# Order of the split products and GpSimd's share of the low weights in the first output projection

## The chip, the cores and the metric

One core of a Trainium2 chip runs the whole program. The metric is the device time of one execution in microseconds (us), as the median of several runs.

## What is computed

The reference is a chain of three blocks over 1024 tokens of width 1024. The change lies at the end of the first block, in its output projection and what follows it:

```python
y = jnp.concatenate([y_conv, y_ret], axis=-1) @ w_out[l]      # 1024 x 2048 by 2048 x 1024
h = h + gate * y
...
return _rmsnorm(h, final_g)
...
h = layer_norm(x, ln_in_g, ln_in_b)                           # first line of the second block
```

All of it is in float32. The kernel gets float32 accuracy out of a faster matmul format (`fp32r`, here F32R) by splitting each operand x in a high part, x rounded to F32R, and a low part, x minus the high part. A product is then the sum of three: high by high, high by low, low by high.

## The kernel before

The stage is `out_sync`, `out_tensor`, `out_scalar` and `out_vector`, one function for each engine's queue. The 2048 rows of `w_out` are taken in 16 pieces of 128 rows (NK = 16), the retention half first (`K_ORDER`). The tokens are 8 tiles of 128, in three groups: (0, 1, 2), (3, 4, 5), (6, 7). Each token tile has a pair of PSUM banks for its 128 x 1024 sum, so only three can be open, and the weights are read once for each group.

A step i of group g multiplies one piece of weights with the group's tokens. `products` (line 369) issues three matmuls for a token and half of the columns, so a step has 18 matmuls in the first two groups and 12 in the third: 768 in all. There are 48 steps, but the last two pieces of a group are kept for the first two steps of the next. So 44 rows of weights are fetched and split, numbered s = 16g + i - 2g. Rows 0 to 15 serve the first group, 14 to 29 the second, 28 to 43 the third.

A row n passes through four engines:
- SyncE fetches it into `wo_raw[:, n % 2]` (line 1306), one of two slots, once the low part of row n-2 is made.
- ScalarE makes `wo_hi` (line 1422) when the row has landed and TensorE is done with row n-2 (`wo_used`).
- VectorE makes `wo_lo` (line 1293, `out_lows`) from `wo_raw` and `wo_hi`.
- TensorE waits at the start of the step for `wo_lo` of its row, and so has the high part too.

In the first group ScalarE and VectorE also split the activations (lines 1424 and 1298).

When a token's sum is complete (`o1_mm`), VectorE multiplies it with the gate into `tmp` (line 1474) and adds it to the residual in `xo` (line 1476). The first step of the next group writes over the banks, each token's after the `tmp` that read it (`gate_ok`). ScalarE takes squares (1450), VectorE normalises: lines 1479, 1483, 1485 for the first norm and the statistics of the second, 1489 and 1494 for centring and scaling. These run beside the next group's steps. Between them VectorE calls `out_lows(dve, upto)`, and ScalarE `highs(upto)`, at places written out by hand. The order of the work on each engine is this order in the code. In steps 10, 11 and 12 of a group TensorE also transposes the finished tokens of the group before (line 1358). ScalarE (1431) and VectorE (1500) take them out of the bank as high and low part for the second block, and SyncE stores the tokens (1313) and loads new residuals (1309) in between.

GpSimd does nothing in this stage. Its next work is `ch_lo` (line 1690), the low part of the weights of the second block's first projection. TensorE's first product of it (`channel`) follows right behind the last step.

## Time and profile before

| | |
|---|---|
| runs | 2764.33, 2764.53, 2764.77 us; median 2764.53 |
| profiled execution | span 2763.9 us from the first to the last instruction; what its run took in all is not listed, the median stands 0.6 us above its span |
| TensorE busy | 2689.4 us, 97% of the span |
| VectorE, ScalarE, GpSimd busy | 2086.6, 1069.2, 477.0 us |
| the stage | first matmul with `wo_hi` at 849.9, first product of the next stage at 1042.2 |

Matmuls overlap in the trace: one is listed with 0.39 us and the next begins 0.23 us later. Starts are more telling than durations.

### The profile page before, as it was taken

Reading aid. Unit: us, or ns where it says so; the run is one execution under the profiler, and the core shown is the slowest. Engines: PE = TensorE matmul, PEld = TensorE weight load, DVE = VectorE, ACT = ScalarE, POOL = GpSimd, SP = SyncE. Lnnn points to the kernel's source line nnn. Section 1 sums busy time; section 2 is a strip of 40 time slices with the busy share of each in tenths; the row PEclk is TensorE's granted clock in tenths of the full one; section 3 lists DMA queues with packets and bytes.
Section 4 is the critical chain, followed back from the end, with each engine's and each line's share of the span. In section 5 each row is a group of like instructions: output and inputs, shape, how many; then the busy total and the mean of one; then the engine's idle time right before and its main releaser. Section 6 shows DMA issues by size and latency. Waiting matters only on the chain.

```text
span 2763.9 us, 33573 instructions
## 1 busy us (share of the span) xinstructions
PE 2689.4 (97%) x13192; PEld 2199.6 (80%) x13192; DVE 2086.6 (75%) x2796; ACT 1069.2 (39%) x1599; POOL 477.0 (17%) x254
## 2 busy tenths in 40 slices
PE   6999999999999999999999999999999999999998
PEld 5888888888888878778875678888887888888887
DVE  6999998873724663369998886688186988887978
ACT  5111112243413332245537751365232554555332
POOL 0000000000100002001210001354211656655000
PEclk8999999999999999999999999999999999999999
DMA  5312222224325452011101032100132222225431
GB/s 223 116 63 69 94 97 61 84 92 142 99 107 175 136 176 90 31 62 39 47 30 36 32 123 96 46 31 23 62 115 80 96 77 89 87 77 188 170 99 61
DMA packets 97710, 250.18 MB, mean 91 GB/s; under 512 B 7361, under 2 KB 34369, under 8 KB 96018
## 3 DMA queue, kind: packets, MB, share of 16 engines
q1 hardware_dynamic: 93010, 231.49, 24.4%
q10 hardware_dynamic: 4288, 15.73, 1.5%
q8 instruction: 105, 1.72, 0.2%
q0 software_dynamic: 256, 0.82, 0.1%
q14 instruction: 51, 0.42, 0.1%
HBM read 202.92 MB, written 45.09 MB: 90 GB/s over the span
## 4 chain that ended last, share of the span: by engine, by line
PE 80%; DVE 14%; issue 2%; ACT 1%; DMA 1%; DVEq 0%; ACTq 0%
PE pair L370 16%; PE pair L372 16%; PE pair L371 16%; PE pair L3657 7%; PE pair L3242 5%; PE pair L3244 5%; PE pair L3245 5%; DVE counted L1942 3%; PE pair L2593 2%; DVE reached L1993 1%; PE pair L2156 1%; DVE top_i L1999 1%; PE pair L1754 1%; PE pair L2172 1%; PE pair L2185 1%
## 5 line engine op out<-in xcount | busy, mean ns | idle before, releaser
L370 PE MATMUL pair<-u_hi,w_hi 128*128 128x512 f32 x768 | 302.1, 393 | 1.2 <-PEq L92 0.9
L641 DVE SCALAR_TENSOR_TENSOR conv_acc<-aT,cols,conv_acc 128x1024 f32<-128x1024 f32 x232 | 297.9, 1284 | 6.7
L371 PE MATMUL pair<-u_lo,w_hi 128*128 128x512 f32 x768 | 300.3, 391 | 0.0
L372 PE MATMUL pair<-u_hi,w_lo 128*128 128x512 f32 x768 | 300.3, 391 | 0.0
L370 PEld LDWEIGHTS pair<-u_hi,w_hi 128*128 128x128 f32 x768 | 145.2, 189 | 32.7 <-issue 2.4
L371 PEld LDWEIGHTS pair<-u_lo,w_hi 128*128 128x128 f32 x768 | 145.0, 189 | 30.6 <-issue 0.7
L372 PEld LDWEIGHTS pair<-u_hi,w_lo 128*128 128x128 f32 x768 | 145.0, 189 | 30.6
L370 PE MATMUL pair<-h_hi,ch_hi 128*128 128x512 f32 x392 | 153.8, 392 | 2.8 <-ACT ch L1824 2.6
L372 PE MATMUL pair<-h_hi,ch_lo 128*128 128x512 f32 x392 | 152.7, 389 | 0.0
L371 PE MATMUL pair<-h_lo,ch_hi 128*128 128x512 f32 x392 | 152.6, 389 | 0.0
L1014 POOL TENSOR_TENSOR yrT<-yrT,gate_c 128x1024 f32<-128x1024 f32 x8 | 18.9, 2366 | 758.1 <-ACT yrT L907 758.1
L3192 POOL TENSOR_TENSOR op_lo<-w_sum,op_hi 128x512 fp32r<-128x512 f32 x80 | 137.6, 1721 | 33.6 <-ACT op_hi L3322 33.6
L454 DVE TENSOR_TENSOR w_lo<-wt,w_hi 128x1024 fp32r<-128x1024 f32 (+1 forms) x64 | 69.8, 1091 | 77.0 <-ACT w_hi L450 76.9
L3242 PE MATMUL pair<-t_hi,op_hi 128*128 128x512 f32 x320 | 124.6, 389 | 0.0
L3245 PE MATMUL pair<-t_hi,op_lo 128*128 128x512 f32 x320 | 124.5, 389 | 0.0
L3244 PE MATMUL pair<-t_lo,op_hi 128*128 128x512 f32 x320 | 124.5, 389 | 0.0
L1690 POOL TENSOR_TENSOR ch_lo<-wt,ch_hi 128x1024 fp32r<-128x1024 f32 x17 | 40.7, 2395 | 464.7 <-ACT ch_hi L1648 464.7
L450 ACT ACTIVATE w_hi<-wt 128x1024 fp32r<-128x1024 f32 (+1 forms) x64 | 60.8, 950 | 142.8 <-PE pair L372 135.3
L1293 DVE TENSOR_TENSOR wo_lo<-wo_raw,wo_hi 128x1024 fp32r<-128x1024 f32 x44 | 54.0, 1228 | 66.5 <-ACT wo_hi L1422 66.4
L370 PE MATMUL pair<-h_hi,p_hi 128*128 128x512 f32 x256 | 103.6, 405 | 0.0
L372 PE MATMUL pair<-h_hi,p_lo 128*128 128x512 f32 x256 | 100.2, 392 | 0.0
L371 PE MATMUL pair<-h_lo,p_hi 128*128 128x512 f32 x256 | 99.7, 389 | 0.0
(510 smaller groups left out, 7105.1 us busy)
## 6 DMA issues: line engine op xcount, KB each, us to landing
wt<-in_w_ch SPq DMA_DIRECT2D x60, 512.0 KB, 3.4
wo_raw<-in_w_out SPq DMA_DIRECT2D x44, 512.0 KB, 3.6
wt<-in_w_up SPq DMA_DIRECT2D x10, 1024.0 KB, 4.9
w_raw<-in_w_up SPq DMA_DIRECT2D x10, 1024.0 KB, 4.8
g_spill<-g_stage SPq DMA_DIRECT2D x40, 256.0 KB, 2.2
ada_mod<-in_ada_mod SPq DMA_DIRECT2D x4, 2048.0 KB, 14.3
wt<-in_w_conv SPq DMA_DIRECT2D x16, 512.0 KB, 3.5
qk<-qk_st SPq DMA_DIRECT2D x8, 1024.0 KB, 6.4
```

Of the source, the lines that this page charges most:

```text
L370: nc.tensor.matmul(bank, w[0], x[0], start=(first and k == 0), stop=False)
L371: nc.tensor.matmul(bank, w[0], x[1], start=False, stop=False)
L372: return nc.tensor.matmul(bank, w[1], x[0], start=False, stop=(last and k == n_k - 1))
L450: nc.scalar.activation(slot_view(w_parts[0], n), slot_view(wt, n), ACT.Copy).then_inc(job_hi, 1)
L454: nc.vector.tensor_tensor(slot_view(w_parts[1], n), slot_view(wt, n), slot_view(w_parts[0], n).bitcast(F32), ALU.subtract).then_inc(job_lo, 1)
L641: nc.vector.scalar_tensor_tensor(dst, x, w, conv_acc[:], ALU.mult, ALU.add).then_inc(conv_step, 1)
L1942: nc.vector.tensor_scalar(to, scores(t), least, None, op, ALU.add, accum_out=found[:, t - 2:t - 1]).then_inc(counts_ok, 1)
L3192: nc.gpsimd.tensor_tensor(op_lo[j], operand(w, j), op_hi[j].bitcast(F32), ALU.subtract).then_inc(op_lo_ok, 1)
L3242: nc.tensor.matmul(bank, hi[:, k, :], x_hi[:, k, :], start=(j in opens and k == 0), stop=False, skip_group_check=True)
L3244: nc.tensor.matmul(bank, hi[:, k, :], x_lo[:, k, :], start=False, stop=False, skip_group_check=True)
L3245: last = nc.tensor.matmul(bank, lo[:, k, :], x_hi[:, k, :], start=False, stop=(k == 3), skip_group_check=True)
L3657: last = nc.tensor.matmul(dn_bank(p, t), x[:, i, t * P:(t + 1) * P], w[:, i, :], start=(p in (P1, P7, P2) and c == kind == i == 0), stop=( ...
```

## The change

Three things are changed:
- In a step TensorE waits for the high part alone. It issues the products with `wo_hi` of all tokens (high and low activations), then waits for the low part, then issues the products with `wo_lo` of all tokens. In the first step of a group this is done token by token.
- The low parts of rows 16 to 29, and of the odd rows 31 to 43, are made by GpSimd (`out_gpsimd`) in place of VectorE, with a semaphore of their own. SyncE waits for the one or the other before it fetches into the slot.
- ScalarE and VectorE take the transposed tokens out of the bank one row of weights earlier.

```diff
--- before.py
+++ after.py
@@ -1284,14 +1284,24 @@
         def x_parts(k):
             return yc_parts if k < KT else yr_parts
 
+        wo_low_pool = sem("o1_wlo_pool")
+
+        def on_pool(n):
+            return NK <= n < NK + NEW or (n >= NK + NEW and n % 2 == 1)
+
+        def wo_low(n):
+            made = sum(on_pool(m) == on_pool(n) for m in range(n + 1))
+            return (wo_low_pool if on_pool(n) else wo_lo_ok), made
+
         at_low = [0]
 
         def out_lows(dve, upto):
             for n in range(at_low[0], min(upto, N_SPLITS)):
                 k = K_ORDER[n % NK]
-                dve.wait_ge(wo_hi_ok, n + 1)
-                nc.vector.tensor_tensor(wo_parts[1][:, n % 2, :], wo_raw[:, n % 2, :],
-                                        wo_parts[0][:, n % 2, :].bitcast(F32), ALU.subtract).then_inc(wo_lo_ok, 1)
+                if not on_pool(n):
+                    dve.wait_ge(wo_hi_ok, n + 1)
+                    nc.vector.tensor_tensor(wo_parts[1][:, n % 2, :], wo_raw[:, n % 2, :],
+                                            wo_parts[0][:, n % 2, :].bitcast(F32), ALU.subtract).then_inc(wo_lo_ok, 1)
                 if n < NK:
                     x = x_parts(k)
                     dve.wait_ge(x_hi_ok, n + 1)
@@ -1302,7 +1312,7 @@
         def out_sync(sp):
             def weights(n):
                 if n >= 2:
-                    sp.wait_ge(wo_lo_ok, n - 1)
+                    sp.wait_ge(*wo_low(n - 2))
                 sp.dma_start(wo_raw[:, n % 2, :], a["w_out"][:, K_ORDER[n % NK], :]).then_inc(wo_in[n % 2], 16)
 
             def residual(t):
@@ -1365,7 +1375,20 @@
                 k = K_ORDER[s % NK]
                 if g and i in (10, 11, 12):
                     transposes(3 * (g - 1) + i - 10)
-                pe.wait_ge(wo_lo_ok, s + 1)
+                x_hi, x_lo = x_parts(k)
+                w_hi, w_lo = (w[:, s % 2, :] for w in wo_parts)
+
+                def multiply(j, t, x, w):
+                    for h in range(2):
+                        last = nc.tensor.matmul(bank_of[j][:, h, :], x[:, k % KT, t * P:(t + 1) * P],
+                                                w[:, h * HALF:(h + 1) * HALF],
+                                                start=(i == 0 and x is x_hi and w is w_hi),
+                                                stop=(i == NK - 1 and w is w_lo))
+                    if i == NK - 1 and w is w_lo:
+                        last.then_inc(o1_mm, 1)
+                    return last
+
+                pe.wait_ge(wo_hi_ok, s + 1)
                 if g == 0:
                     pe.wait_ge(x_lo_ok, i + 1)
                 for j, t in enumerate(O_GROUPS[g]):
@@ -1375,12 +1398,15 @@
                         pe.wait_ge(ot_ok, KT * TT)
                     if n == 0 and j == 1:
                         pe.wait_ge(pw_out, KT - 1)
-                    for h in range(2):
-                        last = products(bank_of[j][:, h, :],
-                                        [x[:, k % KT, t * P:(t + 1) * P] for x in x_parts(k)],
-                                        [w[:, s % 2, h * HALF:(h + 1) * HALF] for w in wo_parts], i, NK)
-                    if i == NK - 1:
-                        last.then_inc(o1_mm, 1)
+                    multiply(j, t, x_hi, w_hi)
+                    multiply(j, t, x_lo, w_hi)
+                    if i == 0:
+                        pe.wait_ge(*wo_low(s))
+                        last = multiply(j, t, x_hi, w_lo)
+                if i:
+                    pe.wait_ge(*wo_low(s))
+                    for j, t in enumerate(O_GROUPS[g]):
+                        last = multiply(j, t, x_hi, w_lo)
                 if i == NK - 1:
                     pe.wait_ge(o1_mm, O_GROUPS[g][-1] + 1)
                     pe.sem_inc(wo_used, 1)
@@ -1459,8 +1485,9 @@
                 act.wait_ge(bnv_ok, tokens[-1] + 1)
                 nc.scalar.activation(sd2, mv1[:, :, 1], ACT.Sqrt, bias=eps5[:]).then_inc(sd_ok, 1)
                 for j, t in enumerate(tokens):
-                    highs(at0 + 12 + j)
+                    highs(at0 + 11 + j)
                     evacuate(t)
+                highs(at0 + 14)
                 if g == 1:
                     act.wait_ge(h2_out[2], 32)
                     channel_high(act, 0)
@@ -1516,7 +1543,7 @@
                 at0 = NEW * (g + 1)
                 if g:
                     for j, t in enumerate(O_GROUPS[g - 1]):
-                        out_lows(dve, NEW * g + 12 + j)
+                        out_lows(dve, NEW * g + 11 + j)
                         low_part(t)
                 out_lows(dve, at0 + 2)
                 add(0, tokens[0])
@@ -1683,6 +1710,13 @@
             sp.dma_start(a_row[:], a["a_bs"]).then_inc(a_in, 16)
             for n in range(10, N_CH):
                 channel_weights(sp, n)
+
+        def out_gpsimd(pool):
+            for n in range(N_SPLITS):
+                if on_pool(n):
+                    pool.wait_ge(wo_hi_ok, n + 1)
+                    nc.gpsimd.tensor_tensor(wo_parts[1][:, n % 2, :], wo_raw[:, n % 2, :],
+                                            wo_parts[0][:, n % 2, :].bitcast(F32), ALU.subtract).then_inc(wo_low_pool, 1)
 
         def mix_gpsimd(pool):
             for n in range(N_CH):
@@ -2385,6 +2419,7 @@
         @block.gpsimd
         def _(pool):
             ret_gpsimd(pool)
+            out_gpsimd(pool)
             mix_gpsimd(pool)
```

How the order of instructions moves is shown at three places. First TensorE, last step of the second group (row 29) before: its start with the first token. L370, L371 and L372 are the three products, `o1_wlo` is the semaphore of VectorE's low parts.

```order
L370 MATMUL pair<-wo_hi,yc_hi 128x512 [waits o1_wlo]
L371 MATMUL pair<-wo_lo,yc_hi 128x512
L372 MATMUL pair<-wo_hi,yc_lo 128x512
L370 MATMUL pair<-wo_hi,yc_hi 128x512
L371 MATMUL pair<-wo_lo,yc_hi 128x512
L372 MATMUL pair<-wo_hi,yc_lo 128x512
L370 MATMUL pair<-wo_hi,yc_hi 128x512
```

The same step with the change, up to the first step of the third group. `o1_whi` is the semaphore of the high parts, `o1_wlo_pool` that of GpSimd's low parts, `o1_gate` that of `tmp`.

```order
L1383 MATMUL pair<-wo_hi,yc_hi 128x512 [waits o1_whi]
L1383 MATMUL pair<-wo_hi,yc_hi 128x512
L1383 MATMUL pair<-wo_hi,yc_lo 128x512 x2
L1383 MATMUL pair<-wo_hi,yc_hi 128x512 x2
L1383 MATMUL pair<-wo_hi,yc_lo 128x512 x2
L1383 MATMUL pair<-wo_hi,yc_hi 128x512 x2
L1383 MATMUL pair<-wo_hi,yc_lo 128x512 x2
L1383 MATMUL pair<-wo_lo,yc_hi 128x512 [waits o1_wlo_pool]
L1383 MATMUL pair<-wo_lo,yc_hi 128x512 x5
L1383 MATMUL pair<-wo_hi,yc_hi 128x512 [waits o1_mm,o1_gate,o1_whi]
```

A token's six matmuls stood together; now the products with `wo_lo` of all three tokens are the last six of the step.

Second GpSimd's queue, between its last work in the stage before (`yrT`) and the next stage's `ch_lo`, before and with the change.

```order
L1014 TENSOR_TENSOR yrT<-yrT,gate_c 128x8x128 [waits x_in1,ada_in3] x8
L1690 TENSOR_TENSOR ch_lo_674<-wt,ch_hi_677 128x1024 [waits ch_hi]
L1690 TENSOR_TENSOR ch_lo_675<-wt,ch_hi_678 128x1024 [waits ch_hi]
L1690 TENSOR_TENSOR ch_lo_676<-ch_raw,ch_hi_679 128x1024 [waits ch_hi]
L1690 TENSOR_TENSOR ch_lo_674<-wt,ch_hi_681 128x1024 [waits ch_hi]
```

```order
L1014 TENSOR_TENSOR yrT<-yrT,gate_c 128x8x128 [waits x_in1,ada_in3] x8
L1718 TENSOR_TENSOR wo_lo<-wo_raw,wo_hi 128x1024 [waits o1_whi] x21
L1724 TENSOR_TENSOR ch_lo_674<-wt,ch_hi_677 128x1024 [waits ch_hi]
L1724 TENSOR_TENSOR ch_lo_675<-wt,ch_hi_678 128x1024 [waits ch_hi]
L1724 TENSOR_TENSOR ch_lo_676<-ch_raw,ch_hi_679 128x1024 [waits ch_hi]
```

The 21 low parts stand ahead of the first `ch_lo`.

Third VectorE in the third group, from row 30 on, beside the normalisation of tokens 3 and 4, before and with the change.

```order
L1293 TENSOR_TENSOR wo_lo<-wo_raw,wo_hi 128x1024 [waits o1_whi]
L1528 RECIPROCAL small_616<-small_616 128x3 [waits o1_rms]
L1479 SCALAR_TENSOR_TENSOR xo_611<-xo_611,small_616,fg_bc 128x1024 [waits o1_rr]
L1483 BN_STATS small_616<-xo_611 128x6 [waits o1_rmsx]
L1483 BN_STATS small_616<-xo_611 128x6
L1485 BN_AGGR small_616<-small_616 128x2 [waits o1_bn]
L1293 TENSOR_TENSOR wo_lo<-wo_raw,wo_hi 128x1024 [waits o1_whi]
L1479 SCALAR_TENSOR_TENSOR xo_612<-xo_612,small_616,fg_bc 128x1024
```

```order
L1303 TENSOR_TENSOR wo_lo<-wo_raw,wo_hi 128x1024 [waits o1_whi]
L1555 RECIPROCAL small_616<-small_616 128x3 [waits o1_rms]
L1506 SCALAR_TENSOR_TENSOR xo_611<-xo_611,small_616,fg_bc 128x1024 [waits o1_rr]
L1510 BN_STATS small_616<-xo_611 128x6 [waits o1_rmsx]
L1510 BN_STATS small_616<-xo_611 128x6
L1512 BN_AGGR small_616<-small_616 128x2 [waits o1_bn]
L1506 SCALAR_TENSOR_TENSOR xo_612<-xo_612,small_616,fg_bc 128x1024
```

The low part of row 31 is gone from between the two tokens.

## Rows read from the trace of the kernel before

**Rows 1.** The page: span, and TensorE's granted clock in 40 slices.

```profile
span 2763.9 us, 33573 instructions
...
PEclk8999999999999999999999999999999999999999
```

**Rows 2.** Windows: us, busy us (x instructions) per engine, clock, DMA share, GB/s.

```profile
822.00:846.00 24.00, 24.00 (x105) 19.39 (x104) 8.13 (x7) 4.97 (x5) 0.00 (x0) 1.00 0.42 145
930.00:956.00 26.00, 26.00 (x117) 21.52 (x116) 18.89 (x21) 7.70 (x8) 0.00 (x0) 1.00 0.48 133
...
985.80:1042.10 56.30, 49.39 (x217) 37.69 (x216) 42.08 (x43) 22.27 (x27) 2.41 (x1) 1.00 0.52 159
```

**Rows 3.** Waits in the third group, 985.8 to 1042.2: us, times, longest.

```profile
ACT wo_hi L1422 <- DMA wo_raw<-in_w_out: 23.6, 11, 3.5
...
PEld pair L370 <- DVE wo_lo L1293: 8.3, 8, 2.0
...
PE pair L370 <- DVE wo_lo L1293: 4.8, 7, 1.5
```

**Rows 4.** Timeline of TensorE: start, us, operation, idle before it.

```profile
916.70 0.47 PE L370 MATMUL pair<-wo_hi,yc_hi 128*128 128x512 f32 x1 [0.30 <-PE pair L372]
...
920.23 0.50 PE L370 MATMUL pair<-wo_hi,yc_hi 128*128 128x512 f32 x1 [0.55 <-DVE tmp L1474]
...
986.12 0.47 PE L370 MATMUL pair<-wo_hi,yc_hi 128*128 128x512 f32 x1 [0.30 <-PE pair L372]
...
996.61 0.50 PE L370 MATMUL pair<-wo_hi,yc_hi 128*128 128x512 f32 x1 [1.53 <-DVE wo_lo L1293]
...
1042.16 0.47 PE L370 MATMUL pair<-h_hi,ch_hi 128*128 128x512 f32 x1
```

**Rows 5.** The chain of waits in order of time: start, us, what.

```profile
983.13 1.24 DVE tmp L1474
...
985.75 1.24 DVE tmp L1474
...
995.46 1.09 DVE wo_lo L1293
...
1019.86 6.00 DMA wo_raw<-in_w_out
```

**Rows 6.** Timeline of ScalarE: high parts of rows 17, 18, 31, 33 and 43.

```profile
926.08 1.06 ACT L1422 ACTIVATE wo_hi<-wo_raw 128x1024 fp32r<-128x1024 f32 x1 [1.67 <-PE pair L372]
930.16 1.06 ACT L1422 ACTIVATE wo_hi<-wo_raw 128x1024 fp32r<-128x1024 f32 x1 [3.02 <-PE pair L372]
...
992.27 1.05 ACT L1422 ACTIVATE wo_hi<-wo_raw 128x1024 fp32r<-128x1024 f32 x1
...
1000.10 1.06 ACT L1422 ACTIVATE wo_hi<-wo_raw 128x1024 fp32r<-128x1024 f32 x1 [3.46 <-DMA wo_raw<-in_w_out]
...
1036.11 1.06 ACT L1422 ACTIVATE wo_hi<-wo_raw 128x1024 fp32r<-128x1024 f32 x1 [1.51 <-PE pair L372]
```

**Rows 7.** Timeline of SyncE: fetches of rows 33 and 43.

```profile
996.58 0.33 SPq L1306 DMA_DIRECT2D wo_raw<-in_w_out  x1
...
1032.09 0.33 SPq L1306 DMA_DIRECT2D wo_raw<-in_w_out  x1
```

**Rows 8.** Timelines of ScalarE, GpSimd and VectorE around the first `ch_lo` operations.

```profile
1031.61 1.05 ACT L1648 ACTIVATE ch_hi<-wt 128x1024 fp32r<-128x1024 f32 x1
...
1032.74 2.41 POOL L1690 TENSOR_TENSOR ch_lo<-wt,ch_hi 128x1024 fp32r<-128x1024 f32 x1 [255.27 <-ACT ch_hi L1648]
1043.19 2.41 POOL L1690 TENSOR_TENSOR ch_lo<-wt,ch_hi 128x1024 fp32r<-128x1024 f32 x1 [8.05 <-ACT ch_hi L1648]
...
1043.31 1.23 DVE L1474 TENSOR_TENSOR tmp<-pair,gate_bc 128x1024 f32<-128x1024 f32 x1
1044.57 2.11 DVE L1476 TENSOR_TENSOR xo<-xo,tmp 128x1024 f32<-128x1024 f32 x1
```

## Prediction

> **What bounds the kernel now.** I read the page first: TensorE is busy nearly everywhere and its clock is granted in full, 2.4 GHz, outside the first slice [rows 1]. So a gain has to come from moments in which TensorE waits, and a loss from new ones. The change touches one stage, 849.9 to 1042 us. The windows by group of tokens come next [rows 2]: in the third group TensorE is busy 49.4 of 56.3 us. A step of three tokens takes 4.08 us, read off ScalarE's pace in the second group, 926.08 to 930.16 [rows 6], so a matmul costs 4.08/18 = 0.227 us. The second group waits for nothing once it runs.
>
> The list of waits of the third group [rows 3] names two limits. TensorE waits for VectorE's low weights, 8.3 us in 8 waits on its weight-load side, and ScalarE's high parts wait for the weights' DMA, 23.6 us in 11 waits. The chain of waits [rows 5] shows how they join. It runs through VectorE's additions from 983.13 on, through its normalisation with a low part in it at 995.46, and later through transfers of `wo_raw` such as the one of 6.00 us at 1019.86. A row n can be fetched only when the low part of row n-2 is made, since both use one slot of `wo_raw`. One turn of a slot is therefore fetch, high part, low part, and two slots alternate. Undisturbed a turn costs 3.5 + 1.1 + 1.2 = 5.8 us [rows 6 to 8], while TensorE needs a slot every 2 x 12 x 0.227 = 5.4 us in the third group and every 8.2 us in the second. In the third group the loop of a slot is the bound, not the moment at which TensorE looks at the low part.
>
> **The change part by part.** The sum is made against the profiled execution, whose span is 2763.9 us. The median of the runs is 2764.5, so 0.6 us lie around the span, and a difference carries over unchanged.
>
> (1) High products first in a step. The matmuls are as many as before. In the steady second group it gives nothing, as TensorE does not wait there. It costs something in the last step of a group. Before, the first token's sum is complete after 6 matmuls of that step; now after 12 + 2 = 14, since the low products of all tokens come last. VectorE's additions begin 8 x 0.227 = 1.8 us later.
> - Into the second group: TensorE's third token starts at 920.23 on the release by VectorE's `tmp` [rows 4], and VectorE needs 2.6 us for each addition pair (983.13 to 985.75, [rows 5]) against TensorE's 1.36 for a token. That start moves by the whole **1.8 us**, and the second group has no slack to take it up.
> - Into the third group: the same again. TensorE starts at 986.12 [rows 4] and would reach its second token at 987.6. VectorE's second `tmp` ends at 985.75 + 1.2 + 1.8 = 988.8, so TensorE loses 1.2. ScalarE's high part of row 31, at 992.27 [rows 6], stands behind the squares of the added rows and moves by the whole **1.8 us**.
>
> (2) GpSimd makes the low parts of the second group (rows 16 to 29). I cost this at nothing. What covers it: fetch 3.5, hand-over and high part 1.1, GpSimd 2.4 make 7.0 us a turn, against 8.2 that TensorE takes. Where stores share the DMA queues a landing takes up to 6.0 [rows 5] and the turn 9.5; the start of a step may then be 1.3 late against a slack of 2.9 (4.08 less the high part). If that cover were gone it would cost about 1 us in each of two or three steps.
>
> (3) GpSimd makes the odd rows 31 to 43. The odd slot makes six turns from the high part of row 31 (992.27) to that of row 43 (1036.11), 43.8 us [rows 6]. Of these the six landings take 3.5 three times, then 4.3, 5.8 and 4.0, 24.6 in all (first and last: 996.58 to 1000.10 and 1032.09 to 1036.11, [rows 6, 7]). The rest, 19.2 us, is high parts, low parts and VectorE being late, as with row 31: high part done at 993.3, low part at 995.4. With GpSimd the rest is per turn 1.13 from the high part's start to GpSimd's (1031.61 to 1032.74), 2.41 for the operation, and 0.03 to the issue: six times 3.57 = 21.4 [rows 8].
> To this comes a wait that the trace shows in its reverse. VectorE's `xo`, two operands in SBUF, takes 2.11 instead of 1.23 us at 1044.57 and ends where GpSimd's operation, begun at 1043.19, has ended (1045.60) plus 1.1 [rows 8]. So these exclude each other. GpSimd's wait is between 0 and one VectorE operation, 1.2 to 1.3. I take 0.2 per turn, 1.1 us in all, since VectorE is on such operations half of the first turns only and nearly idle in the later ones. Sum 22.5 - 19.2 = **3.3 us** later at row 43. I keep the landings as they are, because the stores and loads beside them remain. If all came in 3.5 the sum falls by 3.6; if the three late ones took 6.0 it grows by 3.9.
> The Trainium skill (GPSIMD Engine Reference, section Elementwise — side-by-side cycle accounting) gives an fp32 addition of 2048 elements as 4497 ns, so as an estimate 2.25 us for 1024. By that figure six turns would be 1.0 us shorter; the trace's own 2.41 for this very shape is used instead.
>
> (4) The end. Before, 6.05 us pass from row 43's high part to the channel products at 1042.16 [rows 4, 6], TensorE being the limit. After, the same queue of GpSimd holds row 43's low part and then `ch_lo` of the next stage: 1.13 + 2.41 + 2.41 + 0.05 = 6.0. So **0**, but with GpSimd in TensorE's place.
>
> (5) VectorE gives up 21 low parts of 1.14 to 1.23 us, up to three of which are now in the chain before 1011. They would bring the even slot forward by 2 to 3 us. Worth nothing, as the odd slot comes last. The earlier evacuations on ScalarE are also worth nothing: TensorE's transposes are followed by work that does not need them.
>
> (6) Pitch of the matmuls. The new order alternates between two banks and stationary matrices. Before, pitches differ between stages by some 3% without a wait: 105 matmuls in 24 us and 117 in 26 [rows 2]. Over 768 matmuls that is 5 us. I take none, since the operands are the same as in the nearest row, and put it into the range.
>
> Sum: 1.8 + 1.8 + 3.3 + 0 = 6.9; the second loss of 1.2 in (1) lies beside the second 1.8. Less a little, because TensorE's last step starts nearer to its data: **6.7 us slower**, 2771.2. All that follows hangs on the transposes behind this stage, so nothing takes it up.
>
> **The rivals.**
> - Handover only (0.20): the landings come in 3.5 as the slot's fetches are spread, or VectorE's lateness in the odd slot was larger than I think. Then 6.7 - 3.6 = 3.1: 2767.6, which is no measurable change. For it: the uncontended landings are all 3.5. Against: the stores still stand beside rows 39 to 43.
> - Faster (0.07): what bounds the third group is only TensorE's look at the low part. It comes 8 x 0.227 = 1.8 us later in a step, and GpSimd takes VectorE's queue out of the loop, so the 8.3 us of waits vanish along with most late landings (3.6), against 3.6 for the handovers: about 8 less, 2756. It decides from the point at which a slot's turn is under 5.4 us. Against: fetch and high part alone are 4.6, and GpSimd's 2.4 make 7.0.
> - Port (0.10): each of GpSimd's operations waits for a whole VectorE operation, and VectorE's additions wait for GpSimd in turn. Six times 1.1 more: 2777.5. For it: 2.11 us for `xo` [rows 8]. Against: from 1015 on VectorE has gaps. The Trainium skill (SBUF — State Buffer, section Who interferes with whom) says that whichever of the two begins second is blocked for the whole instruction, and Perfetto Trace Analysis (section Optimizing Scalar/DVE Operations) that offloading between the two might therefore not help. By that rule this rival holds; the trace agrees with the block, but not yet with how often it strikes.
> - The change moves work but costs nothing (0.03): the handover is hidden because VectorE is sped up elsewhere. 2764.5.
>
> **How the numbers follow.** The forecast has 0.60. I count a difference below 0.2% (5.5 us), about what a measurement of this kernel can tell, as no change: 2759.0 to 2770.0. Of the forecast 0.10 falls under that line. Slower: 0.50 + 0.10 = 0.60. Same: 0.10 + 0.20 + 0.03 = 0.33. Faster: 0.07. The range goes from handover only to 3.3 above the forecast, 2767.0 to 2774.5, and leaves out the faster case, most of the port case and the unchanged one, 0.2 together.
>
> **What would show it.** The third token of the second group starts 1.8 us later than 920.23; the high part of row 31 comes 3.6 later than 992.27; six turns of the odd slot take 47 us, and TensorE's waits in the third group are for GpSimd's `wo_lo` and at the end for `ch_lo`. The channel products start near 1048.8. I am wrong if TensorE's waits in the third group sum to less than before, or if row 43's high part begins before 1039.

## The result and the profile after

| | before | change |
|---|---|---|
| runs, us | 2764.77 median of 15 (2763.94 to 2766.79) | 2770.96 median of 15 (2768.94 to 2772.00) |
| ratio | | 1.0021, 95% interval 1.0014 to 1.0028 |
| profiled execution, span | 2763.9 | 2769.2 |
| high part of row 15 (the last before the first handover) | 908.33 | 908.41 |
| first channel product | 1042.16 | 1046.39 |
| from there to the end | 1721.7 | 1722.8 |

The change is 6.2 us slower; 6.7 were forecast. Of the 5.3 us between the two spans 4.2 arise in the stage and 1.1 behind it, where the two kernels have the same code. Every profiled run whose total time is listed took 1.8 us more than its span (2771.01 and 2769.2 for the change). By the same 1.8 us, as an estimate, the profiled execution of the kernel before took 2765.7, 0.9 more than its median, which is why the spans differ by less than the medians.

The page of the change. VectorE has lost 14 us of work and GpSimd gained 54; TensorE is busy 3 us longer, and the span [rows 1] has grown by 5.3.

```profile
span 2769.2 us, 33573 instructions
...
PE 2692.5 (97%) x13192; PEld 2199.6 (79%) x13192; DVE 2072.2 (75%) x2775; ACT 1069.7 (39%) x1599; POOL 530.8 (19%) x275
```

Windows of the change: us, busy us (x instructions) per engine (PE, PEld, DVE, ACT, POOL), clock, DMA share, GB/s. The first three are the three groups of tokens [rows 2]; the last two lie 350 us behind the stage.

```profile
849.90:916.40 66.50, 65.92 (x290) 53.94 (x288) 35.15 (x31) 28.14 (x28) 0.00 (x0) 1.00 0.51 174
916.40:987.60 71.20, 68.83 (x313) 56.31 (x312) 37.83 (x30) 21.53 (x25) 34.50 (x14) 1.00 0.47 148
987.60:1048.50 60.90, 52.97 (x226) 38.89 (x226) 40.76 (x39) 24.93 (x29) 21.93 (x9) 1.00 0.48 156
1392.00:1395.60 3.60, 0.98 (x4) 0.86 (x5) 3.57 (x7) 2.47 (x4) 2.05 (x1) 1.00 0.00 0
1395.60:1399.40 3.80, 3.80 (x11) 2.97 (x10) 3.77 (x10) 2.08 (x4) 0.32 (x1) 0.55 0.00 0
```

Timeline of TensorE in the change: start, us, operation, idle before it. The third token of the second group, the third of the third group, and the first channel product [rows 4].

```profile
922.11 0.74 PE L1383 MATMUL pair<-wo_hi,yc_hi 128*128 128x512 f32 x2 [0.95 <-DVE tmp L1501]
...
990.71 0.73 PE L1383 MATMUL pair<-wo_hi,yc_hi 128*128 128x512 f32 x2 [0.91 <-DVE tmp L1501]
...
1046.39 0.50 PE L370 MATMUL pair<-h_hi,ch_hi 128*128 128x512 f32 x1 [1.14 <-POOL ch_lo L1724]
```

The third token starts 1.88 us later than 920.23. The last row names the new releaser of the next stage, GpSimd's `ch_lo`.

Timeline of ScalarE in the change: high parts of rows 15, 31, 33 and 43 [rows 6].

```profile
908.41 1.06 ACT L1448 ACTIVATE wo_hi<-wo_raw 128x1024 fp32r<-128x1024 f32 x1 [2.07 <-PE pair L1383]
...
995.95 1.05 ACT L1448 ACTIVATE wo_hi<-wo_raw 128x1024 fp32r<-128x1024 f32 x1
...
1003.11 1.06 ACT L1448 ACTIVATE wo_hi<-wo_raw 128x1024 fp32r<-128x1024 f32 x1 [3.08 <-DMA wo_raw<-in_w_out]
...
1040.47 1.06 ACT L1448 ACTIVATE wo_hi<-wo_raw 128x1024 fp32r<-128x1024 f32 x1 [1.77 <-DMA wo_raw<-in_w_out]
```

Row 31's high part is 3.68 us later than 992.27. Six turns of the odd slot take 1040.47 - 995.95 = 44.5 us instead of 43.8; 47 were forecast. Its landings, issue to high part: 3.24, 3.38, 3.35, 4.19, 4.30, 3.96, together 22.4 instead of 24.6.

GpSimd in the change: low parts of rows 31 and 35, then the first `ch_lo` of the next stage, which starts as soon as row 43's low part is out.

```profile
997.08 2.76 POOL L1718 TENSOR_TENSOR wo_lo<-wo_raw,wo_hi 128x1024 fp32r<-128x1024 f32 x1 [13.92 <-ACT wo_hi L1448]
...
1011.57 2.39 POOL L1718 TENSOR_TENSOR wo_lo<-wo_raw,wo_hi 128x1024 fp32r<-128x1024 f32 x1 [4.54 <-ACT wo_hi L1448]
...
1043.96 2.38 POOL L1724 TENSOR_TENSOR ch_lo<-wt,ch_hi 128x1024 fp32r<-128x1024 f32 x1
```

Waits of the third group in the change, 987.6 to 1048.5: us, times, longest [rows 3].

```profile
POOL wo_lo L1718 <- ACT wo_hi L1448: 43.3, 7, 13.9
ACT wo_hi L1448 <- DMA wo_raw<-in_w_out: 21.7, 12, 3.1
...
PEld pair L1383 <- POOL wo_lo L1718: 5.3, 7, 0.9
...
PEld pair L1383 <- ACT wo_hi L1448: 3.4, 6, 1.4
PEld pair L1383 <- DVE wo_lo L1303: 2.7, 3, 1.1
```

TensorE's weight loads (PEld) wait 5.3 + 3.4 + 2.7 = 11.4 us, where they waited 8.3 for VectorE alone: the wait for a low part has become one for low and high parts, and ScalarE still waits for the DMA.

### The profile page after: what moved, and what is told of

The parts are those of the page before. It is cut to its first block, busy times and chain, and to the rows that moved or that the text cites. A ratio compares the mean times of both kernels' runs of the same rounds, so it can differ in the third digit from the quotient of the medians.

```text
span 2769.2 us, 33573 instructions
## 1 busy us (share of the span) xinstructions
PE 2692.5 (97%) x13192; PEld 2199.6 (79%) x13192; DVE 2072.2 (75%) x2775; ACT 1069.7 (39%) x1599; POOL 530.8 (19%) x275
## 4 chain that ended last, share of the span: by engine, by line
PE 83%; DVE 10%; issue 2%; ACT 1%; DMA 1%; POOL 1%; DVEq 0%; ACTq 0%
PE pair L370 16%; PE pair L372 15%; PE pair L371 15%; PE pair L3692 7%; PE pair L3280 5%; PE pair L3277 5%; PE pair L3279 5%; PE pair L1383 4%; DVE counted L1976 2%; PE pair L2628 2%; PE pair L2190 1%; DVE reached L2027 1%; PE pair L1788 1%; DMA wo_raw<-in_w_out 1%; PE pair L2206 1%
## 5 line engine op out<-in xcount | busy, mean ns | idle before, releaser
L370 PE MATMUL pair<-u_hi,w_hi 128*128 128x512 f32 x768 | 302.0, 393 | 1.2 <-PEq L92 0.9
L371 PE MATMUL pair<-u_lo,w_hi 128*128 128x512 f32 x768 | 300.3, 391 | 0.0
L372 PE MATMUL pair<-u_hi,w_lo 128*128 128x512 f32 x768 | 300.1, 391 | 0.0
L370 PEld LDWEIGHTS pair<-u_hi,w_hi 128*128 128x128 f32 x768 | 145.1, 189 | 32.7 <-issue 2.4
L371 PEld LDWEIGHTS pair<-u_lo,w_hi 128*128 128x128 f32 x768 | 145.1, 189 | 31.0 <-issue 0.7
L372 PEld LDWEIGHTS pair<-u_hi,w_lo 128*128 128x128 f32 x768 | 145.0, 189 | 30.2
L370 PE MATMUL pair<-h_hi,ch_hi 128*128 128x512 f32 x392 | 154.5, 394 | 3.8 <-ACT ch L1858 2.7
L372 PE MATMUL pair<-h_hi,ch_lo 128*128 128x512 f32 x392 | 153.3, 391 | 0.0
L371 PE MATMUL pair<-h_lo,ch_hi 128*128 128x512 f32 x392 | 153.1, 391 | 0.0
L370 PE MATMUL pair<-h_hi,p_hi 128*128 128x512 f32 x256 | 103.6, 405 | 0.0
L372 PE MATMUL pair<-h_hi,p_lo 128*128 128x512 f32 x256 | 100.2, 391 | 0.0
L371 PE MATMUL pair<-h_lo,p_hi 128*128 128x512 f32 x256 | 99.6, 389 | 0.0
L370 PE MATMUL pair<-w_o_hi,h_hi 128*128 128x512 f32 x248 | 98.0, 395 | 0.2
L371 PE MATMUL pair<-w_o_lo,h_hi 128*128 128x512 f32 x248 | 96.5, 389 | 0.0
```

Source lines behind the costliest of these rows:

```text
L370: nc.tensor.matmul(bank, w[0], x[0], start=(first and k == 0), stop=False)
L371: nc.tensor.matmul(bank, w[0], x[1], start=False, stop=False)
L372: return nc.tensor.matmul(bank, w[1], x[0], start=False, stop=(last and k == n_k - 1))
```

## The experiments

Each run is compared with the kernel before on the same chip. An interval of a ratio is about 0.001 wide to each side, 2.7 us, so the medians of e3, e5 and e7 can't be told from the kernel before. So besides the medians I read each profiled execution in two pieces: **stage**, from row 15's high part to the first channel product (it takes out that executions enter up to 1.8 us apart), and **behind**, from there to the end of the span. The last two columns count the stretches in which the windows show TensorE's clock below 1.00 in each piece; the last microseconds of the span, without a matmul, are left out.

| run | median minus before, us | stage | behind | low clock in stage | behind |
|---|---|---|---|---|---|
| before / once more (e10) | 0 / 0.0 | 133.8 / 133.3 | 1721.7 / 1721.3 | 0 / 0 | 1 / 1 |
| change / once more (e9) | 6.2 / 5.7 | 138.0 / 139.8 | 1722.8 / 1723.1 | 0 / 0 | 2 / 2 |
| e1 no GpSimd | 3.6 | 135.9 | 1722.1 | 0 | 1 |
| e2 GpSimd only | 3.9 | 135.8 | 1721.8 | 0 | 1 |
| e3 last step by token | 1.6 | 135.5 | 1721.4 | 1 | 1 |
| e4 GpSimd in 2nd group only | 3.8 | 137.8 | 1724.3 | 1 | 2 |
| e5 half of GpSimd's columns | 0.0 | 132.9 | 1724.0 | 0 | 2 |
| e6 delay only | 5.5 | 137.7 | 1721.2 | 0 | 1 |
| e7 third buffer | -0.7 | 131.8 | 1722.8 | 0 | 2 |
| e8 token order, third buffer | -4.5 | 129.1 | 1723.1 | 0 | 2 |
| e11 change, third buffer | 2.8 | 134.5 | 1723.5 | 1 | 2 |
| e12 token order, two buffers | -2.8 | 132.1 | 1721.1 | 0 | 1 |

The starts of the high parts of rows 15, 31 and 43 divide the stage of each profiled execution further. The six turns between the last two are split again into landings and rest, where the two buffers alternate.

| run | row 15 to row 31, us | rows 31 to 43, six turns | of these landings | rest | row 43 to first channel product |
|---|---|---|---|---|---|
| before / once more | 83.9 / 83.9 | 43.8 / 43.3 | 24.6 / 24.1 | 19.3 / 19.1 | 6.05 / 6.07 |
| change / once more | 87.5 / 87.6 | 44.5 / 46.3 | 22.4 / 23.4 | 22.1 / 22.9 | 5.92 / 5.92 |
| e1 no GpSimd | 87.5 | 43.8 | 24.5 | 19.3 | 4.55 |
| e2 GpSimd only | 84.3 | 44.7 | 23.0 | 21.7 | 6.74 |
| e3 last step by token | 84.0 | 45.5 | 23.6 | 21.8 | 6.10 |
| e4 GpSimd in 2nd group only | 87.5 | 44.2 | 25.1 | 19.1 | 6.06 |
| e5 half of GpSimd's columns | 87.6 | 40.5 | 24.9 | 15.6 | 4.83 |
| e6 delay only | 86.6 | 45.1 | 25.9 | 19.2 | 6.10 |
| e7 third buffer | 83.9 | 41.8 | | | 6.06 |
| e8 token order, third buffer | 83.9 | 39.7 | | | 5.50 |
| e11 change, third buffer | 87.5 | 41.0 | | | 5.94 |
| e12 token order, two buffers | 83.9 | 43.5 | 24.2 | 19.3 | 4.64 |

The first column is 3.6 us longer in every run whose last steps have the low products of all tokens at the end (change, e1, e4, e5, e11). The rest of the turns is 19.1 to 19.3 us where VectorE makes the low parts of the third group, and 21.7 to 22.9 where GpSimd makes the odd ones in full.

**e1: the new order without GpSimd.** `on_pool` returns False for every row.

```diff
-            return NK <= n < NK + NEW or (n >= NK + NEW and n % 2 == 1)
+            return False
```

> The change without GpSimd: all low parts on VectorE, products and evacuations as in the change. Theory (handover and slot loop): the two handovers still delay VectorE by 1.8 us each, GpSimd's longer turns and its queue at the end are gone. The high part of row 31 starts 3.6 later than before (995.9), the channel products at 1044.2 (+2.0 against 1042.2 before, -2.2 against the change). Rival (all of the loss is GpSimd's): channel products at 1042.2 or earlier. Rival (all of it is the product order): 1046.4, as in the change.

Median 2768.93 (2767.80 to 2770.22), ratio 1.0012 (1.0003 to 1.0021). First channel product 1044.62, stage 2.3 us over the mean of before (133.5). That is less than the two delays of 1.8: both are there in full (87.5 against 83.9 to row 31), the turns are as long as before, and 1.5 us come back behind row 43's high part (4.55 against 6.05). There TensorE begins the last step on the high part, without the low one. The median moved by 3.6, 1.3 more than this one stage.

**e2: GpSimd alone**, with the products and the places of the high and low parts of before.

```diff
-                pe.wait_ge(wo_hi_ok, s + 1)
+                pe.wait_ge(*wo_low(s))
...
-                    multiply(j, t, x_hi, w_hi)
+                    for h in range(2):
+                        last = products(bank_of[j][:, h, :],
...
```

> GpSimd makes the same rows as in the change, but TensorE waits for the low part at the start of a step and multiplies token by token, as before. Theory: no handover loss, so the third token of the second group starts at 920.2 and the high part of row 31 at 992.3 to 993.3; the odd slot's turns and the queue at the end cost 2.9: channel products at 1045.1. Rival (the loss is the product order's): 1042.2.

Median 2769.21 (2766.38 to 2770.67), ratio 1.0011 (1.0002 to 1.0021). First channel product 1042.78, but it entered 1.3 us earlier: stage 2.2 over. In the stage the two halves of the change cost about the same, 4.5 together, where the change costs 4.4 to 6.3. But the profiled execution of e2 is the fastest of its ten; by the medians the halves cost 3.6 and 3.9, 7.5 together, more than the change's 5.7 to 6.2. How the loss divides is known only to within such differences.

**e3: the last step of a group token by token**, GpSimd as in the change.

```diff
-                    if i == 0:
+                    if i in (0, NK - 1):
...
-                if i:
+                if 0 < i < NK - 1:
```

> The change with one thing undone: in the last step of a group the low products stand behind each token's high products, as in the first step. Theory: both handovers return to 913.7 and 983.1 for VectorE's first addition and the third token of the second group to 920.2; high part of row 31 at 992.3; channel products 3.6 earlier than in the change, 1042.8. Rival (the handover is hidden and the wait moved only): 1046.4.

Median 2766.91 (2765.93 to 2768.30), ratio 1.0002 (0.9993 to 1.0012). VectorE's first `tmp` of the third group comes 69.4 us after that of the second, as before (983.13 - 913.71), against 71.2 in the change (986.81 - 915.60). One edit of two conditions takes back 4.1 to 4.6 us of the 5.7 to 6.2 in the medians, and the whole 3.6 of the first column. That this delay sits in the low products being last is shown. The stage as a whole is 2.5 to 4.3 us shorter than the change's, since the turns differ by up to 0.9 either way.

**e4: GpSimd in the second group only.**

```diff
-            return NK <= n < NK + NEW or (n >= NK + NEW and n % 2 == 1)
+            return NK <= n < NK + NEW
```

> The change, but GpSimd makes only rows 16 to 29; the odd rows of the third group are VectorE's. Theory: GpSimd's work in the second group costs and gives nothing, so every time is that of the kernel without GpSimd within 0.3 us: channel products at 1044.2. VectorE's two-operand operations in the second group stretch from 1.3 to up to 3.5 us and nobody waits. Rival (exclusion of VectorE and GpSimd delays the normalisation into the transposes): later than without GpSimd by over 0.5 us.

Median 2769.09 (2768.36 to 2772.64), ratio 1.0013 (1.0004 to 1.0023): 0.2 over e1, and both pass from row 15 to row 31 in 87.54 us, so GpSimd's 14 rows of the second group are free. The first channel product at 1046.48 missed the expected 1044.2. A stretch at the lower clock falls into the end of the stage, right after a wait, and the last column has 6.06 us instead of e1's 4.55. Windows of this run:

```profile
1036.00:1039.00 3.00, 0.81 (x4) 0.35 (x2) 0.00 (x0) 1.02 (x1) 1.47 (x1) 0.98 0.74 291
...
1040.00:1043.00 3.00, 3.00 (x10) 2.29 (x10) 1.52 (x2) 1.06 (x1) 0.00 (x0) 0.62 0.00 0
```

**e5: half of GpSimd's columns.** In the odd rows from 31 on, the low parts of the other half of the columns are left out.

```diff
-                    nc.gpsimd.tensor_tensor(wo_parts[1][:, n % 2, :], wo_raw[:, n % 2, :],
+                    c = D if n < NK + NEW else HALF
+                    nc.gpsimd.tensor_tensor(wo_parts[1][:, n % 2, 0:c], wo_raw[:, n % 2, 0:c],
```

> The changed kernel, in which GpSimd makes only the first half of the columns of the low weights of the odd rows from 31 on; the low parts of the second half of their columns are left out, so each of those operations should take about 1.2 us instead of 2.40. Theory A (the chain landing, high by ScalarE, low by GpSimd, next transfer paces the third group and bounds the channel stage's start): the six turns from row 31's high to row 43's high lose 6 to 7 us of the 44.5, the first channel product begins 4.2 to 4.9 us earlier than the changed kernel's 1046.39 (at the same entry into the stage; 1041.5 to 42.2), where the in-order even slot or TensorE itself then bounds it. Theory B (only the order of the products costs time): the start stays within 0.5 of 1046.4. Median by A: 2766.5, by B 2771.

Median 2765.55 (2764.44 to 2767.57), ratio 1.0000 (0.9991 to 1.0009). GpSimd in this run, rows 35 and 43, and the first channel product:

```profile
1009.18 1.39 POOL L1719 TENSOR_TENSOR wo_lo<-wo_raw,wo_hi 128x512 fp32r<-128x512 f32 x1 [4.84 <-ACT wo_hi L1448]
...
1036.63 1.29 POOL L1719 TENSOR_TENSOR wo_lo<-wo_raw,wo_hi 128x512 fp32r<-128x512 f32 x1 [4.95 <-ACT wo_hi L1448]
```

```profile
1040.32 0.50 PE L370 MATMUL pair<-h_hi,ch_hi 128*128 128x512 f32 x1 [0.41 <-POOL ch_lo L1725]
```

The stage is 5.1 us shorter than the change's. GpSimd's duration stands in the loop of the odd slot, so theory A holds, but the six turns lose 4.0 (40.5 instead of 44.5), not 6 to 7. All that is not landing falls by 6.5 (22.1 to 15.6), as expected; the landings grow by 2.5 (22.4 to 24.9), one of them to 5.73 (1023.52 to 1029.25). Landings got longer as the other work of the turn got shorter. A further 1.1 us of the gain lie behind row 43's high part (4.83 instead of 5.92), where GpSimd's shorter operation stands as well.

**e6: a plain delay.** The kernel before, with the transposes of five tokens issued twice.

```diff
-                for k in range(KT):
+                for k in list(range(KT)) * (2 if t < 5 else 1):
```

> The kernel before, in which TensorE transposes each of the first five tokens twice (40 further transposes of 0.11 us, 4.4 us of plain work; nothing else moves). It asks whether the 1.2 us of the changed kernel that do not come from its stage (a stretch of 3.4 us at 1.2 GHz near 1396 that the kernel before did not have) come from the later time alone. Theory A (they go with the shift of the later work): a stage that ends 3 to 4.5 us later brings such a stretch here too, and the time is the stage's shift and 1 to 1.5 us more. Theory B (they go with what the change itself issues): the clock after the stage is that of the kernel before, and the time is up by the stage's shift alone.

Median 2771.05, spread over 2767.93 to 2775.70, ratio 1.0019 (1.0010 to 1.0028). The profiled execution is one of the fastest (2768.9): stage 4.2 longer, behind it nothing more, the one low-clock stretch now near 1394 instead of 1161. The profiled one shows theory B. The median is 1.3 above this stage's shift, which would suit A, but the other executions have no trace, so it isn't known whether their time lies in the stage or behind it. The question stays open to that extent. In the stage the delay did more than shift: the landings of the odd rows sum to 25.9 us, the longest of all.

**e7: a third buffer of loaded rows**, before otherwise, except that the unused output of ScalarE's squares goes to a PSUM bank to make room.

```diff
-        wo_raw = at(181, "wo_raw", [P, 2, D])
+        wo_raw_2, wo_raw_3 = at(181, "wo_raw", [P, 2, D]), at(117, "wo_raw3", [P, D])
+        def slot(n):
+            return n % 2 if n < 16 else (n + 1) % 3
...
-                    sp.wait_ge(wo_lo_ok, n - 1)
+                    sp.wait_ge(wo_lo_ok, n - 1 if n < 17 else n - 2)
...
-                    nc.scalar.activation(junk1[:], xo[j][:], ACT.Square,
+                    nc.scalar.activation(flat(pair[1]), xo[j][:], ACT.Square,
```

> The kernel before with a third buffer for the loaded rows of weights from row 16 on (in the place of the output of ScalarE's squares, which goes to PSUM instead). Theory A (the kernel before too is paced in the third group by the turn of its two buffers, transfers included): the transfers start earlier, ScalarE's high of row 43 comes 2 to 3 us before its 1036.1, the first channel product 2 to 2.5 us before 1042.16, median 2762.5. Theory B (the stores and residuals that share the DMA engines set the landings, whenever they start): within 0.5 of 2765.

Median 2764.84 (2763.84 to 2765.26), ratio 0.9996 (0.9987 to 1.0005). The stage is 1.8 us shorter, all of it in the turns of rows 31 to 43, so the turn of two buffers did bound the kernel before. But two low-clock stretches lie behind instead of one, and the median gains only 0.7. Waits of its third group:

```profile
ACT wo_hi L1430 <- PE pair L372: 22.6, 11, 3.5
...
PEld pair L370 <- DVE wo_lo L1301: 8.0, 8, 1.9
```

ScalarE no longer waits for the DMA (23.6 us in [rows 3]) but for TensorE to free a slot of parts, and TensorE's wait for the low part is what it was.

**e12 and e8: the order by itself, freed of its costs.** Both are the change with e1's and e3's edits together; e8 adds e7's buffer, with the wait of SyncE one row further back.

```diff
-                    sp.wait_ge(*wo_low(n - 2))
+                    sp.wait_ge(*wo_low(n - 2 if n < 17 else n - 3))
```

> The changed kernel without GpSimd's part and with the last step of each group token by token (high, low input, low weights), two buffers as before. Theory A (the new order by itself, freed of its two costs, gains, since a step needs its low row only after two thirds of its products): first channel product 1.2 to 2 us before 1042.16 at the same entry, median 2763.5 to 2764.5. Theory B (the order gains nothing; only the third buffer does): within 0.5 of 1042.16, median 2765.5.

> The changed kernel without GpSimd, with the last step of each group token by token (high, low input, low weights) and with the third buffer of the run before. Theory A (the new order is worth something once the wait for low weights and the transfers' turn are both off the path, since each step then needs the low row only after two thirds of its products): first channel product 4.5 to 5.2 us before 1042.16, median 2760.5, faster than both kernels. Theory B (TensorE is the bound as soon as one of the two is gone): as the run with the third buffer alone, 2762.5.

e12: median 2762.77 (2761.95 to 2764.80), ratio 0.9991 (0.9982 to 1.0000), stage 1.5 shorter. e8: median 2761.12 (2760.02 to 2762.79), ratio 0.9983 (0.9974 to 0.9992), stage 4.5 shorter. Theory A holds in both; e8 is faster than the kernel before by 4.5 us and than the change by some 10. Waits of e12's third group, then of e8's:

```profile
ACT wo_hi L1448 <- DMA wo_raw<-in_w_out: 20.4, 12, 3.5
...
PEld pair L1383 <- DVE wo_lo L1303: 5.3, 6, 1.3
...
PEld pair L1383 <- ACT wo_hi L1448: 3.6, 5, 1.2
```

```profile
ACT wo_hi L1456 <- PE pair L1391: 11.5, 6, 2.7
...
PEld pair L1391 <- DVE wo_lo L1311: 5.2, 5, 1.3
...
ACT wo_hi L1456 <- DMA wo_raw<-in_w_out: 1.7, 1, 1.7
```

TensorE's weight loads wait for low parts 5.3 us instead of 8.3, but in e12 another 3.6 for high parts, 8.9 together: while the transfers pace the loop, the order saves nothing in it. The turns of e12 are as long as before (43.5), and its 1.5 us all lie behind row 43's high part (4.64 against 6.05). With three buffers the order is worth 4.5 - 1.8 = 2.7, and of these 2.1 do lie in the turns (39.7 against e7's 41.8). e12's gain is at the edge of its interval; e8's is clear of it.

**e11: the change with the third buffer.**

> The changed kernel as it is, GpSimd included, with the third buffer for the loaded rows. Theory A (with the transfers' turn gone, the chain high by ScalarE, low by GpSimd, free low buffer, next high still costs the odd rows, and the handovers their 1.8 each): about 1.5 us off the changed kernel, first channel product near 1045 at the same entry (2.5 to 3.7 behind the kernel before), median near 2769. Theory B (GpSimd's 2.4 us cost only because the next transfer waits for them): the six turns fall back under the 43.8 us of before, first channel product at 1042 or earlier, median 2766 or less.

Median 2768.33 (2766.53 to 2772.30), ratio 1.0012 (1.0003 to 1.0022). Stage 3.5 shorter than the change's first execution, though a low-clock stretch fell into it; the expectation of A, 1.5, was too low. B was right for the turns, which fell to 41.0, under the 43.8 of before. It missed the first channel product (1043.13 instead of 1042) because the handovers' 3.6 us stay (87.5 in the first column). Against e8, without GpSimd, the turns are 1.4 us longer; how much of that is the stretch of low clock isn't told apart.

**e9 and e10: both kernels once more.**

> The changed kernel once more, unedited, for a second profiled execution. Theory A (the 1.2 us behind the stage belong to single executions: TensorE's stretches at 1.2 GHz fall in other places each time, and how many there are varies): the channel products begin again near 1046.4 (4.2 behind the kernel before, at the same entry into the stage), but the stretches near 1174 and 1396 are elsewhere or differ in number. Theory B (they are tied to this kernel's timing): stretches at the same places, the span again 5.3 above 2763.9.

> The kernel before once more, unedited. It has one such stretch between 100 and 2750 us in its trace (at 1170.7 of the clock's records). Theory A: another place or another number in this execution, with the first channel product still at 1042.2 within 1 us. Theory B: the same single stretch near 1170.

The change again: median 2771.21 (2769.44 to 2773.42), ratio 1.0020 (1.0011 to 1.0030); its profiled execution took 2773.42. The stage is 1.8 us longer than in the first, all of it in the six turns: 1.0 in landings, 0.8 in the rest. One place is row 35's low part; here are GpSimd and VectorE of this execution:

```profile
1012.18 3.43 POOL L1718 TENSOR_TENSOR wo_lo<-wo_raw,wo_hi 128x1024 fp32r<-128x1024 f32 x1 [4.81 <-ACT wo_hi L1448]
```

```profile
1012.10 4.59 DVE L1521 SCALAR_TENSOR_TENSOR xo<-xo,small,lb_bc 128x1024 f32<-128x1024 f32 x2
```

Two VectorE operations of 1.27 us take 4.59 and GpSimd's 3.43 instead of 2.39. In the first execution the same two took 4.48 while GpSimd's took its 2.39. What differs in the rows is who began: there GpSimd's at 1011.57, before VectorE's at 1011.75; here VectorE's at 1012.10, before GpSimd's at 1012.18. The stretches of low clock come at the same two places as in the change's first execution, about 1.6 us later, which was theory B. In the kernel before there is again one, but near 1460 instead of 1161, which was theory A. So the number agreed in both pairs, the place only in one.

## Why the prediction was right, and where it was off

The forecast, 2771.2 (2767.0 to 2774.5), held the time, 2770.96, and the likeliest case was the one that came. Neither sign of being wrong appeared: TensorE's waits in the third group grew, and row 43's high part began at 1040.47, after 1039. Point by point:

- **What was read of the kernel before.** The prediction's "its clock is granted in full" was read off digits that say 90% or more: the windows show one stretch below full clock in it, near 1161, 118 us behind the first channel product. And the 0.6 us between span and median isn't what a run adds to its span, which is 1.8; the difference of the two kernels is not touched by it.
- **(1) The two handovers, 1.8 each.** Right: +1.88 at the third token, +3.68 at row 31's high part (3.60 counted from row 15's). e3 removes them. What the prediction gave away is the other side of the order: the last step of the stage begins without its low part. With VectorE making the low parts that is worth 1.5 us (e1 and e12, last column). In the change GpSimd's longer operations take it back, so GpSimd costs these 1.4 us at the end besides its turns.
- **(2) GpSimd in the second group: nothing.** Right, e4 minus e1 is 0.2 in the medians and nothing from row 15 to row 31 (with the old order of products, e2, it is 0.4). The Trainium skill's page SBUF — State Buffer (Who interferes with whom) speaks of blocking for a whole instruction. It does occur there: VectorE's operation begun at 929.97 lasts until 1.1 us after GpSimd's, begun at 929.08, has ended (931.48). Nobody waits for VectorE. VectorE's normalisation in the second group of the change, where these took 1.28 us before:

```profile
929.97 2.60 DVE L1506 SCALAR_TENSOR_TENSOR xo<-xo,small,fg_bc 128x1024 f32<-128x1024 f32 x1
934.05 2.60 DVE L1506 SCALAR_TENSOR_TENSOR xo<-xo,small,fg_bc 128x1024 f32<-128x1024 f32 x1
```

- **(3) The odd slot, +3.3.** This is the term that was mis-sized: +0.7 in the first execution, 46.3 - 43.8 = +2.5 in the second. Its rest (high, hand-over, GpSimd, its waits) was forecast at 22.5 and measured 22.1 and 22.9, against 19.3 before. The failed step is "I keep the landings as they are": they fell from 24.6 to 22.4 and 23.4. They did so in e2 and e3 too (23.0 and 23.6), while the six executions with VectorE's low parts there have 24.1 to 25.9. So the stage of the first execution (4.2) lies nearer to the rival "handover only" (3.1) than to the forecast, and that of the second is the forecast. SyncE's issues of rows 40 to 43 in the change show how [rows 7]:

```profile
1023.35 0.33 SPq L1316 DMA_DIRECT2D wo_raw<-in_w_out  x1
...
1028.65 0.33 SPq L1316 DMA_DIRECT2D wo_raw<-in_w_out  x1
...
1031.32 0.33 SPq L1316 DMA_DIRECT2D wo_raw<-in_w_out  x1
...
1036.51 0.33 SPq L1316 DMA_DIRECT2D wo_raw<-in_w_out  x1
```

  An odd row is now fetched 5.2 to 5.3 us after the even one and the next even one 2.7 behind it, where before they alternated every 3.9 to 4.2. The odd rows land in 4.30 and 3.96, the even ones in 5.62 and 6.33 (1023.35 to 1028.97, 1031.32 to 1037.65). The even slot has the longer landings, and it isn't the late one. In e5, with shorter turns, row 41 lands in 5.73 again. That this phase is the cause is read from the rows; no run changed it alone.
- **(4) The end, 0.** Right against the kernel before: 1046.39 - 1040.47 = 5.92 us against 6.05, with GpSimd's `ch_lo` as releaser, as said. That the order alone would have gained 1.5 here was not seen.
- **(5) VectorE's relief, nothing.** No run tests it apart. The rest of the turns, 21.7 to 22.9 us around the forecast's 22.5, shows no clear gain.
- **(6) Pitch, nothing.** Right where rows show it: 290 matmuls in 66.5 us against 105 in 24 [rows 2].
- **The port rival** holds in single operations (2.76 and 2.78 in the first execution; 2.77, 2.54 and 3.43 in the second) and not in the later turns, all 2.39 to 2.41: 0.8 and 1.6 us, not six times 1.1.
- **Not foreseen: 1.1 us behind the stage.** In the sum, "nothing takes it up" was taken as "nothing adds to it". The windows of the change at 1392 to 1399.4 show it. The same work in the kernel before:

```profile
1388.00:1391.60 3.60, 1.03 (x5) 0.88 (x6) 3.57 (x7) 2.43 (x4) 2.09 (x1) 1.00 0.01 2
1391.60:1395.40 3.80, 3.80 (x18) 3.17 (x17) 3.77 (x10) 2.08 (x4) 0.28 (x1) 1.00 0.00 0
```

  18 matmuls went through in 3.8 us at 2.4 GHz there, 11 in the change at mostly 1.2 GHz. Seven at 0.23 us are 1.6.

So that the total came within 0.5 us of the forecast is partly luck. The stage was forecast at 6.7 more and took 4.4 more in one execution and 6.3 in the other, against the mean of before (4.2 in the pair compared first). Behind it a second stretch at 1.2 GHz added 1.1 in the first. The mechanism that was forecast, two handovers and a slower odd slot, is what the runs show.

## What to carry to other kernels

When a step's products are regrouped by operand, look at the last step of a group: whoever waits for the first result waits for the whole regrouped step, and keeping that one step in result order takes the cost back. Before moving work to a slower engine, write down the loop it stands in (fetch, high, low, next fetch); the longer operation is paid there even if the engine is idle otherwise (2.4 to 3.6 us in six turns here, of which shorter landings gave back a part). Try a further buffer together with the new order: it was worth 1.8 us of the stage alone and 3.0 beside the order. Look also at where a reordered step gains, which here was its very last one. An effect of a few us should be measured in the stage itself, from its entry to its exit, because the clock behind it can add or hide one or two.

## What was not expected of the hardware

**Stretches at 1.2 GHz behind the stage.** Fourteen profiled executions of twelve kernels run the same work behind the first channel product. Those with one such stretch there took 1721.1 to 1722.1 us, those with two 1722.8 to 1724.3. The means of the two groups are 1.8 us apart. The 21 stretches fall at four places of the same work, counted from the first channel product: 8 at 116 to 119 us, 9 at 347 to 350, 3 at 416 to 419 and one at 522. So the places belong to the work, and which of them is hit changes from execution to execution, in the kernel before even without an edit (118 and 416). The ones shown here follow or begin in a window in which TensorE idles 1.8 to 2.6 us: the change at 1392, e4 at 1036, and these, in e11 inside its stage and in the second execution of before.

```profile
1008.00:1012.00 4.00, 1.97 (x5) 1.62 (x6) 3.96 (x5) 2.19 (x3) 1.00 (x1) 0.79 0.23 92
1010.00:1014.00 4.00, 3.97 (x10) 3.13 (x11) 4.00 (x3) 0.93 (x1) 3.00 (x1) 0.57 0.21 29
```

```profile
1455.00:1459.00 4.00, 2.23 (x12) 1.02 (x12) 3.47 (x9) 3.02 (x8) 0.00 (x0) 0.97 0.89 273
...
1459.00:1463.00 4.00, 4.00 (x23) 2.31 (x22) 1.40 (x6) 2.77 (x12) 0.00 (x0) 0.61 0.14 57
```

A wait isn't sufficient: at 1388 to 1391.6 the kernel before idles 2.6 of 3.6 us and keeps its clock, while the change idles as long at 1392 to 1395.6 and loses it. What decides between them stays open.

**Landings go with the moments of their issues.** The same 512 KB rows land in 3.2 to 8.1 us (3.24 for row 33 in the change, 8.07 for row 42 in its second execution). With VectorE's low parts (before twice, e1, e12) row 41 lands in 5.3 to 5.8 us and row 42 in 5.3 to 5.5. With GpSimd's (change twice, e2, e3) they take 4.3 to 4.8 and 6.1 to 8.1. e4 and e6 have 4.6 and 6.4, and 6.0 and 7.1, without GpSimd there, so GpSimd's part isn't needed for such a shift. Shortening the turn (e5) gave back 2.5 us of 6.5 in longer landings, and lengthening it (the change) returned 2.2 and 1.2.
